# Position biases reversed as eight short runs while two norms wait, instead of as sixteen full rows during the projections

## The reference

```
x = x + (1 + g1) * conv_mixer(rms_norm(x) * (1 + sc1) + sh1)
x = x + (1 + g2) * (square(relu(h @ mlp_w1)) @ mlp_w2)            # h = the second norm, modulated
proj = h @ w_in                                                     # second block: h = norm 2 of this text
...
bias = rpb[:, rr, rc]                                               # 8 heads, 15 x 31 entries a head
s = einsum(q, k[:, idx]) * scale + bias[None]
p = softmax(s)
...
return rms_norm(x, final_w)
```

## Time and profile before

| | us |
|---|---|
| median of three runs | 2604.91 (2602.04 to 2606.07) |
| the profiled execution | 2602.53 |
| its span in the profile | 2600.4 |
| TensorE busy | 2510.2 (97%) |
| VectorE busy | 1780.5 (68%) |
| ScalarE busy | 1142.0 (44%) |
| GpSimd busy | 374.2 (14%) |
| granted TensorE clock, mean | 0.992 of 2.4 GHz |

### The profile page before, as it was taken

How to read it: one execution, slowest core, us unless ns; L and a number is a source line. 1 busy time by engine, 2 the same in 40 slices (tenths; PEclk the granted TensorE clock), 3 DMA queues, 4 the chain that set the end, 5 groups by cost and what they waited for, 6 DMA issues and landing times.

```text
span 2600.4 us, 29532 instructions
## 1 busy us (share of the span) xinstructions
PE 2510.2 (97%) x10860; PEld 1969.3 (76%) x10860; DVE 1780.5 (68%) x2148; ACT 1142.0 (44%) x1438; POOL 374.2 (14%) x177
## 2 busy tenths in 40 slices
PE   4889999999999999999999999999999999999998
PEld 2344557887888888888888888788888888888886
DVE  5679958678778779877754556695676654555455
ACT  2155445543443443444554454444544334443444
POOL 1069652022122222221000000000000000000000
PEclk9999999999999999999999999999999999999999
DMA  8999747598898888887554557885688766666664
GB/s 312 376 381 381 257 152 247 175 324 299 313 304 306 301 290 305 310 302 266 170 169 147 154 162 259 275 303 193 186 284 276 249 192 193 187 189 192 192 188 138
DMA packets 332510, 643.45 MB, mean 247 GB/s; under 512 B 21328, under 2 KB 55792, under 8 KB 331344
## 3 DMA queue, kind: packets, MB, share of 16 engines
q1 hardware_dynamic: 331104, 640.89, 74.6%
q0 software_dynamic: 448, 0.43, 0.1%
q10 hardware_dynamic: 816, 0.26, 0.0%
HBM read 639.40 MB, written 2.10 MB: 247 GB/s over the span
## 4 chain that ended last, share of the span: by engine, by line
PE 84%; DVE 9%; DMA 4%; ACT 2%; SPq 1%; issue 0%; POOL 0%; DVEq 0%; ACTq 0%; POOLq 0%
PE bank L88 84%; DVE bank L88 5%; DMA stage<-in_mod_w 3%; DMA stage<-in_mlp_w 1%; DVE R L88 1%; DVE acc L88 1%; ACT whi L88 1%; DVE R2f L88 1%; DVE wlo L88 1%; SPq L88 1%; ACT hhi L88 0%; DVE X L88 0%; ACT scr L88 0%; DVE scr L88 0%; POOL wlo L88 0%
## 5 line engine op out<-in xcount | busy, mean ns | idle before, releaser
L88 DVE TENSOR_TENSOR wlo<-stage,whi 128x1024 fp32r<-128x1024 f32 x688 | 855.3, 1245 | 588.6 <-ACT whi L88 568.7
L88 ACT ACTIVATE whi<-stage 128x1024 fp32r<-128x1024 f32 x752 | 795.2, 1059 | 977.9 <-PE bank L88 868.2
L88 PE MATMUL bank<-whi,hhi 128*128 128x512 f32 x2016 | 802.3, 398 | 17.5 <-DVE wlo L88 8.8
L88 PE MATMUL bank<-whi,hlo 128*128 128x512 f32 x2016 | 787.2, 390 | 0.0
L88 PE MATMUL bank<-wlo,hhi 128*128 128x512 f32 x2016 | 786.6, 390 | 0.0
L88 PEld LDWEIGHTS bank<-whi,hhi 128*128 128x128 f32 x2016 | 379.7, 188 | 101.2 <-ACT scr L88 10.2
L88 PEld LDWEIGHTS bank<-whi,hlo 128*128 128x128 f32 x2016 | 379.5, 188 | 80.6
L88 PEld LDWEIGHTS bank<-wlo,hhi 128*128 128x128 f32 x2016 | 379.9, 188 | 77.8 <-issue 0.7
L88 PE MATMUL bank<-whi,uhi 128*128 128x512 f32 x992 | 390.0, 393 | 0.6 <-ACT whi L88 0.6
L88 PE MATMUL bank<-whi,ulo 128*128 128x512 f32 x992 | 390.1, 393 | 0.0
L88 PE MATMUL bank<-wlo,uhi 128*128 128x512 f32 x992 | 387.8, 391 | 0.0
(11 more groups left out here) (127 smaller groups left out, 1170.6 us busy)
## 6 DMA issues: line engine op xcount, KB each, us to landing
stage<-in_mlp_w SPq DMA_DIRECT2D x256, 512.0 KB, 5.6
stage<-in_mod_w SPq DMA_DIRECT2D x192, 512.0 KB, 9.3
stage<-in_w_ada SPq DMA_DIRECT2D x192, 512.0 KB, 5.1
stage<-in_w_in SPq DMA_DIRECT2D x136, 512.0 KB, 3.9
stage<-in_w_ffn_gate SPq DMA_DIRECT2D x88, 512.0 KB, 4.3
stage<-in_w_ffn_up SPq DMA_DIRECT2D x88, 512.0 KB, 3.8
stage<-in_w_ffn_down SPq DMA_DIRECT2D x88, 512.0 KB, 4.2
stage<-in_conv_w_in SPq DMA_DIRECT2D x128, 256.0 KB, 8.8
```

The source lines that it names most:

```text
L88: made = fn(*args, **kw)
```

## The change

The load of the runs is a task of its own and comes earlier: beside the eighth load after the start of conv-out, no longer beside the 24th after norm 1, where only the mask stays. The runs are flipped as they are, before any shift: `flip_runs` makes two matmuls of 438 columns (two heads each) in norm 1 and two in norm 2, in the place of the ten matmuls `bank<-ident,ones`, which stay in norm 3. ScalarE copies each result from its bank back over the run in `R3`. `finish_bias` has no matmul left: VectorE reads the flipped run with the overlapping steps, one addition of 256 columns for each token half. At the end, the second half's reciprocal is written behind the first half's scalings.

```
-                t2 = T.put(nc.tensor.matmul, bank[:, t * S:(t + 1) * S], flip[:, :], shifted_rows(h, t), ...)
-            bias_ready[h] = V.put(tensor_tensor, bias_of(h), bank[:, :]..., mask[:, :, :], ALU.add, after=[t2, tm])
+        def flip_runs(part):
+            two = [misc.take(), misc.take()]
+            w = 2 * N_RUN
+            at = [runs[:, (2 * part + k) * w:(2 * part + k + 1) * w] for k in range(2)]
+            t = [T.put(nc.tensor.matmul, two[k][1][:, 0:w], flip[:, :], at[k], start=True, stop=True,
+                       after=[runs_in[0], flips] + two[k][2]) for k in range(2)]
+            for k in range(2):
+                r = A.put(nc.scalar.activation, at[k], two[k][1][:, 0:w], ACT.Copy, after=[t[k]])
+                misc.give(two[k][0], r)
+        def finish_bias(h):
+            for t in range(2):
+                rows = bass.AP(runs.tensor, runs.offset + h * N_RUN + 62 * (1 - t), [list(runs.ap[0]), [31, 4], [1, 64]])
+                bias_ready[h] = V.put(nc.vector.tensor_tensor, bias_of(h)[:, t, :]..., rows, mask[:, t, :]..., ALU.add,
+                                      after=[run_rows[h], runs_in[1], marks["gates_read"], marks[("w2", 3)]])
...
-            for _ in range(N_WARM): ...
+            if n < 3:
+                flip_runs(n - 1)
+            else:
+                for _ in range(N_WARM): ...
...
+        beside[loaded_upto[0] + 8] = load_runs
         products(n1, n2)
         norm_phase(1, h2_ready, pe_done[-1])
-        beside[loaded_upto[0] + 24] = load_biases
+        beside[loaded_upto[0] + 24] = load_mask
...
-        r = [rstd_of(tok) for tok in range(2)]
+            r.append(rstd_of(tok))
```

More of the change, by code:

```diff
@@ L1458, in build_program, with load_runs @@
         bias_ready = {}
[L1460 to L1465, removed]
+        runs = R3[:, 0, 0, 0:8 * N_RUN]
+        runs_in, run_rows = [], {}
+        def load_runs():
             ln_b = line("s_rpb")
@@ L1471, in load_biases @@
                 src = bass.AP(a["nat_rpb_2"].tensor, (5 - half) * 31 + 15 - 63, [[1, 64], [465, 8], [1, N_RUN]])
[L1472 to L1486, removed]
@@ L1487, in load_biases, with load_mask @@
-            marks["finish_bias"] = finish_bias
+                t = Y.load(R3[64 * half:64 * half + 64, 0, 0, 0:8 * N_RUN].rearrange("p (h n) -> p h n", h=8), src,
+                           ln_b, after=[marks["bout_read"]])
+            runs_in.append(t)
+        def load_mask():
+            runs_in.append(Y.load(mask[:, :, :], a["window_mask"].rearrange("(t p) n -> p t n", p=128), line("s_mask"),
+                                  after=[ln["taps_done"]]))
+        def flip_runs(part):
[7 more added lines that the diff above has]
+                misc.give(two[k][0], r)
+                for h in (4 * part + 2 * k, 4 * part + 2 * k + 1):
+                    run_rows[h] = r
@@ new lines, in finish_bias @@
+        def finish_bias(h):
+            for t in range(2):
+                rows = bass.AP(runs.tensor, runs.offset + h * N_RUN + 62 * (1 - t), [list(runs.ap[0]), [31, 4], [1, 64]])
+                bias_ready[h] = V.put(nc.vector.tensor_tensor, bias_of(h)[:, t, :].rearrange("p (r c) -> p r c", r=4), rows,
+                                      mask[:, t, :].rearrange("p (r c) -> p r c", r=4), ALU.add,
+                                      after=[run_rows[h], runs_in[1], marks["gates_read"], marks[("w2", 3)]])
+            marks["R3_free"] = marks["R3_free"] + [bias_ready[h]]
@@ L1489, in bias_of @@
+        marks["finish_bias"] = finish_bias
         def bias_of(h):
@@ L1696, in norm_phase @@
                 run_one() if tasks or delayed or slow else consume()
[L1697 to L1701, removed]
+            if n < 3:
+                flip_runs(n - 1)
+            else:
+                b, bank, free = misc.take()
+                for _ in range(N_WARM):
+                    t = T.put(nc.tensor.matmul, bank[:, 0:128], ones[:, :], ident[:, :], start=True, stop=True,
+                              after=[consts] + free)
+                misc.give(b, t)
             turn_quarter(0, made)
@@ L1769, in build_program @@
         ln["taps_done"] = conv_done[NKT - 1]
+        marks["bout_read"] = x_free[0][0]
+        beside[loaded_upto[0] + 8] = load_runs
         products(n1, n2)
         norm_phase(1, h2_ready, pe_done[-1])
-        marks["bout_read"] = x_free[0][0]
         marks["convread"] = s_ready[NKT - 1][1]
-        beside[loaded_upto[0] + 24] = load_biases
+        beside[loaded_upto[0] + 24] = load_mask
         products(n2, n3)
@@ L1802, in build_program @@
         ov = out[0].rearrange("(t p) n -> t p n", p=128)
-        r = [rstd_of(tok) for tok in range(2)]
-        made = {}
+        r, made = [], {}
         for tok in range(2):
             rstd = ST[:, 12 + tok:13 + tok]
+            r.append(rstd_of(tok))
             for q in (3, 2):
```

## The result

| | before | changed |
|---|---|---|
| median | 2606.03 us (22 runs, 2600.91 to 2614.05) | 2599.89 us (22 runs, 2594.0 to 2608.29) |
| ratio | | 0.9975, 95% interval 0.9968 to 0.9982 |
| span of the profiled execution | 2600.4 us | 2599.4 us |

The changed kernel is 6.1 us faster by the medians, 0.25%. The two profiled spans differ by 1.0 us only. Where the other 5 went is the first question that the traces must answer, and one execution of each kernel can't. One run of a later experiment (e6) took 3086.02 us at a mean granted clock of 0.776 and is left out of its ratio.

A forecast was written before the change was run, and what follows sets the result against it. TensorE was taken as the bound, with 84% of the chain that ended last. Flips -7.1, norms 0, load +0.9 and last scaling 0 sum to -6.2 us, from 2604.9 to 2598.7 us; range 2594.5 to 2604.0.

The forecast's parts named there:

- flips out of the projections: Projections: removing the flips between tiles takes 7.1 us off TensorE's path; VectorE's extra additions stay hidden.
- norms: Norms 1 and 2: flips replace fillers and hide in TensorE's wait, ScalarE's copies hide too; 0 us.
- load into conv-out: Conv-out: the moved load takes 2.65 us of DMA, partly covered by lead; +1.5 us, from 0 to 2.65.
- load out of the MLP: MLP: without the load a TensorE stall for a weight tile goes; -0.6 us, at best -2.65, at worst 0.
- last scaling: End of the kernel: nothing that starts the eight stores moves; 0 us, at best -0.2.
- first sign of being wrong: Conv-out: longer by more than 2.65 us would show the forecast wrong.
- 7 x 0.92 + 0.68: Projections: seven pairs of flips at 0.92 us and one behind transposes at 0.68 us, 7.1 us removed.
- Rival C: Norms 1 and 2: the gap left by fewer fillers halves the clock, 2.5 us each; 2603.7 us in all, chance 0.07.
- rival D: Conv-out: three short stalls grow to 3.97 us and slow the clock, 17.0 us; 2615.7 us in all, chance 0.06.
- the price of 2.65 us: The load's DMA time: 0.90 MB at 338 GB/s hold all DMA engines for 2.65 us.
- A, "the move of the load is free": Load drains in conv-out and its time returns in the MLP, -1.3 us; -8.4 in all, 2596.5 us, chance 0.15.
- B (-4.5): Conv-out pays the load's full 2.65 us and the MLP gives nothing; -4.5 in all, 2600.4 us, chance 0.17.

The follow-up runs named there:

- e6: Changed kernel with the load back in the MLP, fillers in norm 1 and all four flips in norm 2; 2598.77 us, ratio 0.9977.
- e8: Changed kernel as it is, run on the same chip and in the same rounds as e7; 2599.01 us, ratio 0.9975.
- e1: Kernel before with only the load of the runs moved beside entry +8 of conv-out; 2606.03 us against 2606.17, ratio 0.9999.
- e9: Same program as e4 once more, nothing in the waits of norms 1 and 2; 2598.7 us in one run.
- a1: Changed kernel executed and profiled a second time, no edit; 2596.99 us, span 2594.9 us.
- e2: Changed kernel with the load beside entry +35 instead of +8, behind the modulation tiles; 2597.97 us, ratio 0.9972.
- e3: Changed kernel with as many bytes loaded as rows of 7008 bytes instead of 876, so other biases; 2600.04 us against 2606.53, ratio 0.9973.
- e7: Same kernel as e2, run beside e8 on the same chip; 2596.99 us, ratio 0.9963.
- e4: Changed kernel without flips and without fillers in norms 1 and 2, biases not reversed; 2601.46 us, ratio 0.9980.
- e5: Changed kernel with the load in the MLP, fillers in all three norms and compact flips as two tasks in the projections; 2603.38 us, ratio 0.9988.
- b1: Kernel before executed and profiled a second time, no edit; 2604.36 us, span 2602.3 us.

## Why the prediction was right

2598.7 us was forecast, -6.2 us; it is 2599.89, -6.1 by the medians of its own rounds, and -5.7 in those of e8. Each term against what was measured:

| term | predicted | measured | by |
|---|---|---|---|
| flips out of the projections | -7.1 | -7.27 | C to D, all executions |
| norms | 0 | 0 | 5.98 us from fill to next stage in norm 1, changed and before |
| load into conv-out | +1.5 (0 to 2.65) | +2.4 (single executions +1.2 to +3.2) | A to norm 1's first `dg` matmul, see below |
| load out of the MLP | -0.6 (-2.65 to 0) | -0.9, unsure | B to C, see below |
| last scaling | 0 | 0 | D to end 939.0 in both |
| sum | -6.2 | -5.8 | medians: -6.1, -5.7 |

The total alone tests no term: its interval is -8.3 to -4.7 us, and the range forecast was 9.5 us wide. The signs that the prediction named are met for the flips and the norms, and the stall at 559 is gone. Its first sign of being wrong, conv-out longer by more than 2.65 us, stood at 2.64 in the profiled execution and at 3.0 in e1 and e9. So the flips were right by their mechanism; that the load's two errors left the sum near its mark is in part luck.

**Flips.** 7 x 0.92 + 0.68 was right to 0.2 us, and the additions took 419 ns where 424 stood in the earlier trace rows: the read with overlapping steps costs nothing more. VectorE has no wait for TensorE on its additions now, and TensorE none for `wlo` in that stretch.

**Norms.** The flip took 1.63 us (1.64 forecast), the gap 0.43 (0.5), the two copies 0.94 (at most 1.19). Rival C put 2.5 us a norm on the clock. In the change it does not happen: the gap of 0.43 us stands in twelve norms of six executions (changed, a1, e8, e2, e3, e7), and the clock stays at 1.00 in all. But its mechanism is real: e4 and e9 show it for a wait of 1.9 us. Two things in the prediction's handling of it were wrong. It was priced at 2.5 us, and the two cases cost 1.0 and 0.6. And rival D was said to decide "from a stall of about 4 us on". From A on, the stalls that halved the clock are those of 1.89 (e9 at 424.66), 1.90 (e9, norm 2), 1.91 (e4, norm 1), 2.06 (e1) and 2.39 us (e5); two waits of 1.91 us did not (e4, norm 2; e9, norm 1), nor did any shorter stall, up to 1.79 us (a1 at 424.27). The one long stall of the earlier trace rows had been read as a threshold, and these traces show none: 3.59 us did not halve the clock in e1, 1.89 us did in e9. The Trainium skill ("TensorE: Matmul & The Clock Gate", Part 1: The HAM clock gate) says that the same kernel shows other counts of slow matmuls from run to run, by the phase of the chip's free-running look at TensorE's activity. By that rule a wait like these is a draw, and e4 against e9 agrees: two executions of one program, 5.75 and 4.15 us for the same row. The same section of the Trainium skill lets the clock fall only behind a long idle stretch, so for the gap of half a microsecond it spoke less for rival C than the prediction said; on the stalls of 1.9 to 2.4 us the measurements decide. The filler's worth is then some 0.6 to 1.0 us in those executions and norms where the draw falls, not what one execution shows.

**The load.** This term was mis-sized, in two places that partly cancel. A to B with the load there averages 94.6 us over five executions (changed 94.79, a1 94.58, e8 93.24, e1 95.12, and e9 95.14, whose norm 1 ran at full clock), and 92.0 over the six without it (before, b1, e2, e5, e6, e7; 91.61 to 92.22). That leaves out e4, whose norm 1 ran slow. From A to norm 1's first `dg` matmul all can be compared: 87.1 us over six executions with the load there (85.90 to 87.94, e4 86.38), 84.8 without (84.27 to 85.04), so +2.4, near the upper end of the forecast. Of this 1.5 us are stalls (3.6 behind A in place of 2.0). Another 0.6 is the clock, half of the time that it stood at 0.50: 2.6 to 2.8 us in four of the six, but 4.3 and 4.5 in e1 and e9, where it fell a second time behind the load's stall. The remaining 0.2 us is spread over the stage. The forecast had the stalls' 1.5 us, but its way to them held a wrong price and no clock. B to C averages 740.5 with the load there (before, b1, e5, and e6 less the 0.85 of its norm) and 739.6 without (eight executions, e4's 738.69 among them), so -0.9; but single ones scatter by 1.7 us, and without e5 (742.98, with a stall of 2.39 us and a halved clock behind the load) the difference is nearly nil. The step that failed is the price of 2.65 us, which took the load at the 338 GB/s of the earlier trace rows. The window from 540 to 550 lay mostly before the load's rows moved. While they move the rate is 199 to 208 GB/s at a DMA share of 1.02 to 1.13. By an estimate from these rows: in 6 us at 199 GB/s 1.19 MB arrive, 0.90 of them the load; the other 0.29 MB would take 0.8 us at the 386 GB/s that conv-out reaches when only tiles are in flight, so the load holds back the stream for 5 us, not 2.65; its packets' own durations give 4.7. Lead and pauses took half of it. The windows 548 to 552, behind the issue, held the right rate in the trace of before.

The Trainium skill ("DMA: Bandwidth & Descriptors", Why small descriptors are slow (HBM only)) puts three cycles on every packet beside one for each 32 bytes. For 876 bytes that is an estimate of 11% by its rule (27.4 + 3 against 27.4), and nearly none for long rows. e3 moved 15% more in the same 6 us, near that, but the durations of the packets differ by more, 83 against 61 ns per 1000 bytes, or 36%. The rest of the gap to 331 GB/s this rule doesn't explain.

**Rivals.** A, "the move of the load is free", was not what the change did (e7 against e8, 2.0 us), but it is what its load does at entry +35: -7.27 + 0 - 0.9 = -8.2 us, or -7.4 without e5's stall, and e2 and e7 measured -8.2 and -7.7. B (-4.5) has nearly the right time for conv-out with nothing back from the MLP; the medians of -6.1 and -5.7 are nearer to the forecast, and the MLP's scatter doesn't exclude B's reason. D did not come: no stall in the three executions of the change was longer than 1.8 us behind the load. In e1, whose load is the same, 2.06 us was enough for the clock to fall, so the margin was small.

## What to carry to other kernels

Where one engine holds the chain for 80% and more, its timeline between fixed instructions gives a change's price to 0.1 us in stages that run without stalls, while two profiled spans of one kernel can be 4.5 us apart; compare the stages, and repeat the execution before believing the rest. Flipping the data before it is shifted and spread out (219 columns a head for 512) was worth more than moving the work into a wait (4.35 against 2.92 us). A load of short rows into part of the partitions should be priced by the rate while it is in flight, and placed where the stream has a pause that no engine's lead depends on; one number in a table (entry +8 to +35) was worth 2 us here.

## What the runs showed of the hardware

- Two fp32 matmuls of 438 columns between tiles cost 1.46 us (e5), 1.67 ns a column, and two of 256 columns 0.92 us, 1.80 ns a column. An estimate from these two: 1.5 ns a column and 0.2 us for the change of matmul kind.
- From A on, stalls of TensorE of 1.9 to 2.4 us halved its granted clock (1.00 to 0.50) in five of seven cases; ahead of it one of 1.95 to 2.22 us did in three of thirteen executions, and one of 3.59 us did not.
- Packets of 876 bytes into 64 partitions took 73 ns each, those of 2048 bytes of the weight tiles 91 ns, so a byte cost 1.9 times as much.
- The DMA share read 1.02 to 1.13, full, at 199 to 208 GB/s while the runs were in flight, and 1.05 at 386 GB/s when only weight tiles were: the share says that the engines are held, not that bytes move.
- The point A, before which the kernels do not differ, came at 406.0 to 412.4 us from execution to execution, a scatter as large as the whole gain.
